# Two blocks in high and low parts on one core: shorter chains at norms and recurrence, token-major gates, alternating order of products

## What is computed

```python
def first_block(x, ...):
    for layer in range(2):
        mix = even_mixer(x, ...) if layer % 2 == 0 else odd_mixer(x, ...)
        x = layer_norm(ALPHA * x + mix, ln1_g[layer], ln1_b[layer])
        x = layer_norm(ALPHA * x + conv_ffn(x, ...), ln2_g[layer], ln2_b[layer])
    return x

def even_mixer(x, w_in, ...):            # HGRN2 recurrence (8 heads, both directions) and a gated MLP
    q, f_fw, f_bw, i_in, g, u, v = jnp.split(x @ w_in, cuts, axis=-1)
    o = hgrn2_bidirectional(q, i_in, f_fw, f_bw, lb)
    o_a = rms_norm(o, a_norm_g) * jax.nn.silu(g)
    o_b = u * (b_ws @ layer_norm(v) + b_bias)
    return jnp.concatenate([o_a, o_b], axis=-1) @ w_out

def second_block(x, ...):
    h = rms_norm_2(x, ln_pre_g)
    rnn_x, rnn_gate, q, k, v, attn_gate, g_rnn, g_attn = split_columns(h @ w_in)
    y_rnn = (rg_lru(rnn_x, ...) * jax.nn.silu(rnn_gate)) @ w_rnn_out
    y_attn = (dilated_attention(q, k, v) * jax.nn.silu(attn_gate)) @ w_attn_out
    merged = jax.nn.sigmoid(g_rnn) * y_rnn + jax.nn.sigmoid(g_attn) * y_attn
    return x + rms_norm_2(merged @ w_o, ln_post_g)
```

## Time and profile before

| | |
|---|---|
| median of 3 runs | 3324.51 us (3318.84 to 3326.64) |
| the profiled execution | 3321.39 us |
| its span, first to last instruction | 3319.6 us |
| TensorE busy | 3277.7 us, 99% |
| VectorE, ScalarE, GpSimd busy | 68%, 42%, 9% |
| mean granted TensorE clock | 0.996 |
| HBM traffic | 184 GB/s over the span |

### The profile page before, as it was taken

One profiled execution on the slowest core, in us unless ns is written; L12 is line 12 of the kernel. 1 busy time (PEld: TensorE's weight loads), 2 busy tenths in 40 slices (PEclk: granted clock), 3 DMA queues, 4 the chain that ended last, 5 costly groups with the idle time before them and its releaser, 6 DMA issues.

```text
span 3319.6 us, 42990 instructions
## 1 busy us (share of the span) xinstructions
PE 3277.7 (99%) x17716; PEld 2842.2 (86%) x17716; DVE 2244.3 (68%) x2217; ACT 1379.4 (42%) x1058; POOL 283.7 (9%) x108
## 2 busy tenths in 40 slices
PE   8999999999999999999999999989999999999999
PEld 7888888888888888888888888878888898888887
DVE  6756677888874465768888884458866566555674
ACT  5534343333333345644333333335733333354433
POOL 1300101111120000000111110000012011000000
PEclk9999999999999999999999999989999999999999
DMA  6555345555555545455555555545555545545554
GB/s 255 203 203 177 123 170 190 188 187 188 188 191 222 193 173 179 140 190 180 189 189 190 191 190 216 194 161 190 188 190 195 194 160 181 190 152 180 202 190 164
DMA packets 88448, 617.27 MB, mean 186 GB/s; under 512 B 10320, under 2 KB 11216, under 8 KB 15312
## 3 DMA queue, kind: packets, MB, share of 16 engines
q1 hardware_dynamic: 83232, 592.34, 49.5%
q10 hardware_dynamic: 5040, 22.35, 1.9%
HBM read 608.36 MB, written 2.10 MB: 184 GB/s over the span
## 4 chain that ended last, share of the span: by engine, by line
PE 93%; DVE 3%; issue 2%; ACT 1%; DVEq 1%; POOLq 0%; DMA 0%; POOL 0%; ACTq 0%
PE acc L309 40%; PE acc L313 21%; PE acc L368 7%; PE acc L367 7%; PE acc L369 7%; PE acc L326 2%; PE acc L327 2%; PE acc L328 2%; DVE w_lo L229 0%; PE acc L1706 0%; PE acc L556 0%; PE acc L1489 0%; PE acc L1487 0%; PE acc L1488 0%; PE acc L1324 0%
## 5 line engine op out<-in xcount | busy, mean ns | idle before, releaser
L229 DVE TENSOR_TENSOR w_lo<-w_raw,w_hi 128x2048 fp32r<-128x2048 f32 x558 | 1360.4, 2440 | 807.1 <-ACT w_hi L225 806.2
L225 ACT ACTIVATE w_hi<-w_raw 128x2048 fp32r<-128x2048 f32 x558 | 1068.3, 1917 | 1577.8 <-PE acc L313 963.1
L309 PE MATMUL acc<-x_hi_lo,w_hi 128*128 128x512 f32 x5952 | 1443.6, 393 | 15.7 <-DVE w_lo L246 8.6
L309 PEld LDWEIGHTS acc<-x_hi_lo,w_hi 128*128 128x128 f32 x5952 | 1094.3, 189 | 229.3 <-issue 18.5
L313 PEld LDWEIGHTS acc<-x_hi_lo,w_lo 128*128 128x128 f32 x5952 | 773.3, 192 | 33.2
L313 PE MATMUL acc<-x_hi_lo,w_lo 128*128 128x256 f32 x5952 | 786.0, 283 | 0.0
L367 PE MATMUL acc<-w_hi,hidden_hi_lo 128*128 128x512 f32 x832 | 324.1, 390 | 0.0
L368 PE MATMUL acc<-w_lo,hidden_hi_lo 128*128 128x512 f32 x832 | 324.1, 390 | 0.0
L369 PE MATMUL acc<-w_hi,hidden_hi_lo 128*128 128x512 f32 x832 | 324.1, 389 | 0.0
L367 PEld LDWEIGHTS acc<-w_hi,hidden_hi_lo 128*128 128x128 f32 x832 | 156.2, 188 | 32.5
L369 PEld LDWEIGHTS acc<-w_hi,hidden_hi_lo 128*128 128x128 f32 x832 | 156.2, 188 | 32.3
(11 more groups left out here) (257 smaller groups left out, 2007.4 us busy)
## 6 DMA issues: line engine op xcount, KB each, us to landing
w_raw<-weights_dram SPq DMA_DIRECT2D x558, 1024.0 KB, 4.8
over<-rows_dram ACTq DMA_DIRECT2D x10, 1024.0 KB, 8.3
over<-over ACTq DMA_DIRECT2D x20, 128.0 KB, 2.4
u_tiles<-x_dram SPq DMA_DIRECT2D x4, 512.0 KB, 8.1
w_raw<-weights_dram SPq DMA_DIRECT2D x4, 512.0 KB, 7.0
resid<-x_tok_dram ACTq DMA_DIRECT2D x1, 2048.0 KB, 8.6
over<-w_gates_dram ACTq DMA_DIRECT2D x1, 2048.0 KB, 8.4
out_dram<-resid SPq DMA_DIRECT2D x8, 256.0 KB, 2.1
```

The source lines that it names most:

```text
L225: act.activation(whi[:, n % NHI, :], raw[:, n % NRAW, :], ACT.Copy).then_inc(weights_hi, 1)
L229: dve.tensor_tensor(wlo[:, n % NRAW, :], raw[:, n % NRAW, :], whi[:, n % NHI, :].bitcast(F32), ALU.subtract).then_inc(weights_split, 1)
L309: pe.matmul(acc[:, 4 * t + f, :], whi[:, n % NHI, tile(f, kk):tile(f, kk) + P], moving(k, 0, 2 * T), start=(k == 0), stop=False)
```

## The change

1. **Kind order.** In feature-major chunks narrow and wide products change places from one chunk to the next (hi lo, lo hi, hi lo ...), and from one part to the next of the first chunks behind a norm. Those begin with w_lo x_hi, and for block 0 TensorE waits only for the high part of the activation. In chunks 0 and 1 of the program the high products of a half chunk run before its low ones and wait only for the half's high part.
2. **Norms.** Groups are (1, 1, 2, 4, 4, 4) blocks in place of (2, 2, 4, 4, 4); the first two pieces of activations are single blocks. For block 0 of the tokens, groups 1 and 2 are scaled before block 1's statistics.
3. **The norm behind down1.** The last three chunks are done block by block, not two. Cast and split of rnn_in's first chunk move behind; the root scale is applied by ScalarE (group_scale), and ln_pre_g with the split of the transposed parts, as a column.
4. **Recurrence.** The mask is loaded in task 3 of mix0_in, in the place of the residual's load, which moves behind the squares of the outputs; prob and the mask lie where the residual goes later, and prob is zeroed before the loop. The first scores wait for two banks read out. Two weight splits move behind the loop over groups.
5. **Last block.** gates, dil_out and rnn_out are token-major. ScalarE takes the sigmoid from PSUM, VectorE multiplies and adds token-major, and TensorE turns the merged sum in four lots of eight transposes, three between the chunks of rnn_out and one in last_out, where the two engines split it from PSUM.
6. **End.** All four output parts of block 0 are finished before block 1's.

The diff, cut to its core:

```diff
-GROUPS = [(0, 2), (2, 2), (4, 4), (8, 4), (12, 4)]
-TURN_BEFORE = {1: 1, 3: 2, 6: 3, 10: 4}
+GROUPS = [(0, 1), (1, 1), (2, 2), (4, 4), (8, 4), (12, 4)]
+PIECES = [(0, 1), (1, 1)] + [(k, 2) for k in range(2, MT, 2)]
+TURN_BEFORE = {1: 2, 3: 3, 6: 4, 10: 5}
...
+                        held = 2 if name == "down1" else 1
+                        if not (last and hold and c >= nch - held) and n + 2 < NCHUNKS:
                             piece(eng, n + 2)
...
+            low_first = bool(before_k)
...
+                        for part, places in enumerate(parts_of(n, first, c)):
                             if first:
+                                for kk in sorted({kk for _f, kk in places}):
+                                    before_k(CK * c + kk)
+                            for low in (low_first, not low_first):
+                                if n < 2:
+                                    pe.wait_ge(((half_hi, weights_hi), (half_split, weights_split))[low][part], n + 1)
+                                elif first and c == part == 0 and not low:
+                                    before_k(0, 1)
+                                weights, depth = (wlo, NRAW) if low else (whi, NHI)
+                                cols = T if low else 2 * T
+                                for f, kk in places:
...
+                            if n >= 2:
+                                low_first = not low_first
...
+        def parts_of(n, first, c):
+            if n < 2:
+                return [[(f, kk) for kk in range(CK) for f in (2 * h, 2 * h + 1)] for h in range(2)]
+            cuts = ((0, 1, 2, CK) if c == 0 else (0, 2, CK)) if first else (0, CK)
+            return [[(f, kk) for kk in range(a, b) for f in range(CF)] for a, b in zip(cuts, cuts[1:])]
...
+                    held = (3 if name == "down1" else 2) if last else 0
...
+        def group_scale(act, g):
+            act.wait_ge(pre_scale, 1)
+            at0, n = group_cols(g)
+            for b in range(2):
+                o = act.activation(u_tok[:, b, at0:at0 + n], part(b, at0, n), ACT.Identity, bias=eps[:, 2:3],
+                                   scale=rst[:, b:b + 1])
+            o.then_inc(x_tok, 1)
...
                 dve.tensor_reduce(moments[:, :, 0], parts[:], AX, ALU.add).then_inc(ln_var, 1)
-                dve_rstd(dve, 9, 0, 2)
-                group_affine(dve, nxt, 0, 0)
-                group_affine(dve, nxt, 0, 1)
+                dve.wait_ge(ln_std, 9)
+                dve.reciprocal(rst[:, 0:2], std[:, 0:2]).then_inc(pre_scale, 1)
+                split_chunk(dve, CHUNK0[nxt])
...
             if c == 1 and task == 3:
-                act.dma_start(z[:], d["x_tok"]).then_inc(z_landed, 16)
+                act.dma_start(flat(bwm[:]), d["con"][:, CON0["bw_mask"]:CON0["bw_mask"] + 4 * P])\
+                   .then_inc(hg["masks"], 16)
...
+                    if task == 13 and f == 1:
+                        o.then_inc(hg["emptied"], 1)
...
                 if g == 1:
                     lo_part(dve, 2, tiles(UU0), READY0["mix0_out"] + 1)
-                else:
-                    split_chunk(dve, CHUNK0["mix0_out"] + g - 1)
+            split_chunk(dve, CHUNK0["mix0_out"] + 1)
             hgrn_take(dve, NG - 1)
             lo_part(dve, 3, tiles(UU0 + 4), READY0["mix0_out"] + 2)
+            split_chunk(dve, CHUNK0["mix0_out"] + 2)
...
+        def act_gates(i, t, task, n):
+            act, q = nc.scalar, 2 * i + t
+            dst = gate_rnn if q < 4 else gate_attn
+            act.wait_ge(chunk_used, n + 1)
+            act.wait_ge(acc_free, task + 2)
+            for b in range(2):
+                o = act.activation(dst[:, b, 512 * (q % 4):512 * (q % 4) + 512], acc[:, 4 * t + b, :], ACT.Sigmoid)
+            o.then_inc(acc_free, 1)
...
+        def merged_turn(pe, q):
+            pe.wait_ge(merged, q + 1)
+            if q >= 2:
+                pe.wait_ge(moving_ready, READY0["last_out"] + q - 1)
+            for f in range(4):
+                for b in range(2):
+                    o = pe.transpose(acc[:, merged_bank(q) + f // 2, (f % 2) * T + b * P:(f % 2) * T + (b + 1) * P],
+                                     gate_rnn[:, b, (4 * q + f) * P:(4 * q + f + 1) * P], ident[:])
+            o.then_inc(merged_turned, 1)
```

328 lines of the change are left out of this document (185 added, 143 removed).

## The result

| | before | changed |
|---|---|---|
| median of 4 runs | 3325.57 us (3318.84 to 3328.25) | 3300.14 us (3298.43 to 3301.02) |
| ratio, 95% interval | | 0.9932 (0.992 to 0.9944) |
| the profiled execution | 3321.39 us | 3300.98 us |
| its span | 3319.6 us | 3299.2 us |
| mean granted clock | 0.996 | 0.998 |

The changed kernel is 25.4 us faster by the medians and 20.4 us by the two profiled spans. The predicted 3303 us was 2.9 us too slow, the range held the time, and the sum of 19.8 us stands against 20.4 measured between the profiles. The other 5 us lie in the kernel before: its profiled execution was one of its shorter ones, and its runs spread over 9 us where those of the changed kernel spread over 2.6.

The account below looks back on a forecast made before the run. TensorE, busy 3277.7 of 3319.6 us, was taken as the bound: its work plus few waits. Terms summed to 19.8 us, giving 3301.6 from the profiled execution or 3304.7 from the median; forecast 3303 us, range 3295 to 3313.

Parts of the forecast that it names:

- Token-major last block: Gates, attention and recurrent projections: 56 chunks at 5.45 in place of 5.57 us, less 3.6 us for transposes; net -3.1 us.
- The rival that a narrow product costs no more for its columns: Last block: both kinds of chunk take the same time there, 3310 us; chance 0.03.
- Alternating order: Feature-major chunks: one change of width per chunk in about 300 chunks saves 0 to 4.5 us; -3.2 us taken.
- The slower rival: Runs of 32 narrow products stretch because weight loads do not keep up: 3377 us, middle 3340; chance 0.05.
- Prologue: Program start: high parts first bring the first product 1.2 us earlier; -0.9 us taken (0.6 to 1.5).
- if full speed comes at the same moment only half is kept: Program start: first products run at half speed, so 0.6 us of the 1.2 us earlier start is kept.
- Recurrence: Three waits go: earlier mask 2.0 us, last values 4.2 us earlier in all, clock fall avoided 1.7 us; -5.9 us.
- Three norms: Behind mix0_out, down0 and attn_out: smaller first pieces, narrow products first, VectorE's queue the next limit; -2.0 us (0 to 4).
- block 6 starts 0.65 us earlier: Three norms: with VectorE's queue as limit, the new order laid out gains 0.65 us per norm, not 1.6.
- The rival of ladders that lose 1.5 us each: Three norms: the new order waits for group 3's transposes, each losing up to 1.5 us; 3309 us; chance 0.07.
- Norm behind down1: Between down1 and rnn_in: chain 2.7 us earlier, reciprocal to first product 2.7 in place of 3.8 us; -3.5 us taken.
- End: Last block: all four parts of block 0 fit VectorE's 2.2 us pause before block 1's; -1.2 us.

Follow-up runs that it names:

- the late case: Executions of the changed kernel in which a weight chunk landed late in mix0_in and TensorE waited in task 5; the profiled 3300.98 us is one.
- experiment 11: The changed kernel once more, without an edit: 3299.09 us; its trace has no wait in mix0_in's task 5 and a span of 3297.4 us.
- experiment 1: The changed kernel with the alternation taken back, every feature-major chunk again 16 wide then 16 narrow products: 3302.90 us.
- experiment 3: The changed kernel with VectorE's two weight splits back inside the recurrence's loop: 3307.00 us.
- experiment 4: The changed kernel with the backward mask loaded at the start of the recurrence, as before, not in task 3 of mix0_in: 3304.55 us.
- experiment 10: The changed kernel with wide products first behind the norms, block 0 waiting for high and low part of its activation: 3301.12 us.
- experiment 9: The changed kernel with the last two chunks of down1 done for block 0 first, not three: 3301.77 us.
- experiment 7: The changed kernel with 46 in place of 16 clock-keeping products of ones behind down1: 3297.62 us.
- experiment 5: The changed kernel with 1 - gate in mix0_in done on VectorE in place of GpSimd: 3298.72 us.
- experiment 12: The changed kernel with 1 - gate on VectorE, block 3's products behind group 3's transposes, 46 clock-keeping products behind down1, 12 products of ones at the start: 3296.36 us.

## Why the prediction was right

**What bounds the kernel** held: the gain is work of TensorE (12.0 us less busy) and its waits (8.4 less), and no other engine took over. That the sum of 19.8 us comes within 0.6 of the 20.4 measured is in part luck. Recurrence, norms and alternation gave 2.1 us more than their terms, and the trace compared with holds 1.3 us of the late case. Against the trace of experiment 11 the gain is 22.2 us, 2.4 more than the sum; the range holds that too.

**Token-major last block** (-3.1, measured -3.3). Chunks take 5.440 us, not the cautious 5.45, and came from 5.567: 0.127 us each in place of 0.12; some 0.2 us of that is missing in gates, at the borders of tasks. The transposes cost 0.9 us for eight as read from the earlier trace rows, and their waits nothing. The rival that a narrow product costs no more for its columns is gone with it. The Trainium skill's page "TensorE: Matmul & The Clock Gate", section "Back-to-back issue gap", gives the isolated gap from which 216 and 109 ns were estimated; the changed trace contradicts it, with 5.440/24 = 0.227 us for a wide product, as the earlier trace rows did.

**Alternating order** (-3.2, measured -3.5, and as much by experiment 1). The excess of a chunk does go with its changes. The value taken between the ends, 0.011 us a chunk, was the measured one (0.0105). It holds for 322 chunks, where some 300 had been taken. The slower rival, narrow products that starve in runs of 32, did not occur: pairs of chunks take 11.113 us throughout.

**Prologue** (-0.9, measured -0.6 in this pair of traces). The first product came 1.15 us earlier as worked out, but the step "if full speed comes at the same moment only half is kept" is what happened, and the moment itself moves from run to run: chunk 0 took 7.0 to 8.4 us in the traces with this start. So the 0.2 to 0.3 added for runs of eight was lost in that.

**Recurrence** (-5.9, measured -6.8). The order of events was right: first scores at 331.67 (331.5 worked out), masking at 333.85 (333.6), last values without a pause, no fall of the clock. One size was off, and for one reason above all. The last values start 4.9 us earlier where 4.2 was taken, because the clock had fallen twice before, not once, and the first fall lies in front of them. I had read the window at 363.8 and not this one of the kernel before:

```profile
336.50:339.90 3.40, 2.93 (x13) 2.93 (x14) 3.25 (x13) 0.00 (x0) 0.00 (x0) 0.50 0.00 0
```

It explains the 3.44 us of the scores at 336.97 in the earlier trace rows, which take 2.02 now. By waits and clock the gain is 4.97 - 1.56 = 3.4 us of pauses and another 3.4 us of two falls (3.4 us each at half speed). The term took all three waits as gone; one of 1.56 us stayed. Experiments 3 and 4 show the same split: of 6.7 us for the splits 1.5 are pause and 5.1 clock, of 3.0 us for the mask 1.6 and 1.4. I had called the 4.2 us an effect of the moved split; by itself the split costs 1.5 us of wait, and the clock makes the rest of it.

**Three norms** (-2.0, measured -2.9). The step that failed in size is "block 6 starts 0.65 us earlier". The first product is 1.4 us earlier (1.6 worked out), and the wait for VectorE came where it was put, at group 3's transposes, but it costs less. Experiment 10 shows a link that the step did not name: an earlier first product also brings the next transposes and so VectorE's next operation forward, by most of its size. That this makes up the whole difference was not measured. The rival of ladders that lose 1.5 us each found its wait, 1.61 us three times, and not its loss.

**Norm behind down1** (-3.5, measured -3.3). 2.7 us from the third chunk held (experiment 9: 2.73), 1.2 from the reciprocal to the first product (3.80 to 2.57), and 0.7 back through ScalarE's queue, as "gives some back" had it. The clock still fell; experiment 7 shows that this was 1.6 us more to be had with 30 products of ones.

**End** (-1.2, measured -1.3).

**Not foreseen**: +1.3 us in mix0_in and +0.4 in attn_out. The first is the late case, which the changed kernel shows in one of its two traces (experiment 11), so it is chance within this kernel; whether the change made it likelier can't be told from one trace of the kernel before. The second is a wait for L1413. It is 0.5 us in the kernel before and in the two kernels with experiment 5's edit (experiments 5 and 12), whose mix0_out is 0.35 us longer instead, and 0.8 in all others; its cause stays open.

**The extra 5 us of the medians.** Seven runs of the kernel before on one chip lie within 2 us (3320.97 to 3322.98), nine on another within 4.2 us (3321.23 to 3325.39), and thirteen on a third spread from 3319.05 to 3327.87 at mean clocks of 0.995 to 0.997. Each fall that lasts 10.2 in place of 3.4 us costs 3.4 us more, and the pauses that let it fall stand in the kernel before at three places. The changed kernel keeps one. That the length of the falls makes the spread is argued from experiment 3, whose runs spread over 7.7 us and part by the clock; in the single runs of the kernel before the places were not seen.

## What to carry over

A pause of TensorE costs itself and the half speed that may follow it. Read the granted clock behind every pause of over a microsecond before pricing it, and fill those that can't be removed with idle products: 30 of them were worth 1.6 us here. And where two engines hand work to each other in turn, a wait on one of them is not slack: trace the order on both before calling an earlier step hidden.
